# Recurrent mixer: per-head sums of squares and spreads as 64x64 products on four quarters of the matrix array

## What is computed

```python
kk = heads(k * k_k)
kk = kk / jnp.maximum(jnp.sqrt(jnp.sum(kk * kk, axis=-1, keepdims=True)), 1e-12)
...
mean = jnp.mean(y, axis=-1, keepdims=True)
var = jnp.mean(jnp.square(y - mean), axis=-1, keepdims=True)
yn = ((y - mean) * lax.rsqrt(var + RWKV_LN_EPS)).reshape(B, S, RWKV_WIDTH)
yn = yn * lnx_w.astype(f32) + lnx_b.astype(f32)
```

## Time and profile before

| what | value |
|---|---|
| time, median of 3 runs | 2650.77 us (2650.51 to 2651.02) |
| profiled execution: span from first to last instruction | 2650.5 us |
| PE / PEld / DVE / ACT busy | 2622.0 / 2259.3 / 1931.6 / 1381.8 us |
| chain that ended last, share of PE | 95% |
| mixer's core, four iterations and the end | about 291 to 449 us |

### The profile page before, as it was taken

How to read it: one execution, slowest core, us unless ns; L and a number is a source line. 1 busy time by engine, 2 the same in 40 slices (tenths; PEclk the granted TensorE clock), 3 DMA queues, 4 the chain that set the end, 5 groups by cost and what they waited for, 6 DMA issues and landing times.

```text
span 2650.5 us, 46085 instructions
## 1 busy us (share of the span) xinstructions
PE 2622.0 (99%) x16930; PEld 2259.3 (85%) x16930; DVE 1931.6 (73%) x2963; ACT 1381.8 (52%) x2153; POOL 148.1 (6%) x162
## 2 busy tenths in 40 slices
PE   9999999999999999999999999999999999999998
PEld 8888888889888888888888888888888888888886
DVE  6778676877877877878887666578877756775676
ACT  6545555676544534435554454345455535553554
POOL 5600002301000000000000000000000000000000
PEclk9999999999999999999999999999999999999999
DMA  7555103555787787878778855677665555555554
GB/s 262 174 192 175 58 4 129 181 186 215 266 300 280 285 296 278 295 281 283 278 274 304 292 177 184 203 275 281 247 206 188 194 192 189 189 194 191 188 193 151
DMA packets 159504, 578.42 MB, mean 218 GB/s; under 512 B 18224, under 2 KB 18768, under 8 KB 158288
## 3 DMA queue, kind: packets, MB, share of 16 engines
q1 hardware_dynamic: 156224, 563.59, 61.3%
q10 hardware_dynamic: 2080, 9.46, 1.0%
q0 software_dynamic: 1008, 2.71, 0.4%
HBM read 572.81 MB, written 2.11 MB: 217 GB/s over the span
## 4 chain that ended last, share of the span: by engine, by line
PE 95%; DVE 2%; issue 1%; ACT 1%; POOL 1%; DMA 0%; SPq 0%; ACTq 0%; DVEq 0%; POOLq 0%
PE ps L2742 34%; PE ps L2746 18%; PE ps L2824 12%; PE ps L2826 12%; PE ps L2825 12%; PE ps L1151 1%; PE ps L1802 1%; PE ps L1164 0%; POOL ssm L1900 0%; DMA raw<-in_stream 0%; DVE wlo L2282 0%; PE ps L1100 0%; PE ps L2808 0%; PE ps L2809 0%; PE ps L2807 0%
## 5 line engine op out<-in xcount | busy, mean ns | idle before, releaser
L2282 DVE TENSOR_TENSOR wlo<-raw,whi 128x1024 fp32r<-128x1024 f32 x872 | 1059.3, 1230 | 516.8 <-ACT whi L1933 514.1
L1933 ACT ACTIVATE whi<-raw 128x1024 fp32r<-128x1024 f32 x871 | 903.3, 1056 | 778.7 <-PE ps L2746 367.9
L2742 PE MATMUL ps<-xn,whi 128*128 128x512 f32 x3760 | 941.3, 392 | 2.7 <-DVE wi L618 1.0
L2742 PEld LDWEIGHTS ps<-xn,whi 128*128 128x128 f32 x3760 | 674.7, 188 | 123.4 <-issue 2.2
L2746 PEld LDWEIGHTS ps<-xn,wlo 128*128 128x128 f32 x3760 | 510.8, 191 | 37.4 <-DVE wlo L2282 0.4
L2746 PE MATMUL ps<-xn,wlo 128*128 128x256 f32 x3760 | 520.6, 282 | 0.0
L2824 PE MATMUL ps<-whi,act_in 128*128 128x512 f32 x1120 | 436.1, 389 | 0.0
L2826 PE MATMUL ps<-whi,act_in 128*128 128x512 f32 x1120 | 435.7, 389 | 0.0
L2825 PE MATMUL ps<-wlo,act_in 128*128 128x512 f32 x1120 | 435.7, 389 | 0.0
L2824 PEld LDWEIGHTS ps<-whi,act_in 128*128 128x128 f32 x1120 | 210.2, 188 | 44.7 <-DVE wlo L2282 1.0
L2826 PEld LDWEIGHTS ps<-whi,act_in 128*128 128x128 f32 x1120 | 210.2, 188 | 43.7
(11 more groups left out here) (344 smaller groups left out, 2233.0 us busy)
## 6 DMA issues: line engine op xcount, KB each, us to landing
raw<-in_stream SPq DMA_DIRECT2D x872, 512.0 KB, 4.2
adaw<-in_ada SPq DMA_DIRECT2D x96, 512.0 KB, 5.8
adaq<-in_ada SPq DMA_DIRECT2D x96, 512.0 KB, 5.0
h<-in_xT SPq DMA_DIRECT2D x8, 256.0 KB, 8.9
memx<-in_memT ACTq DMA_DIRECT2D x1, 2048.0 KB, 9.2
gate_row<-gates POOLq DMA_DIRECT2D x2, 1024.0 KB, 7.6
lwa<-in_lora ACTq DMA_DIRECT2D x2, 512.0 KB, 4.5
lwa<-in_lora ACTq DMA_DIRECT2D x1, 1024.0 KB, 8.6
```

The source lines that it names most:

```text
L1933: act.activation(whi[:, r, :], raw[:, r, :], ACT.Copy).then_inc(hi_done, 1)
L2282: dve.tensor_tensor(wlo[:, r, :], raw[:, r, :], whi[:, r, :].bitcast(F32), ALU.subtract)\
L2742: return pe.matmul(ps[:, lin.bank(g, t), :], whi[:, (p0 + s) % RING, c * 512 + t * P:c * 512 + (t + 1) * P], x[:, 2 * s + c, :], start=s + ...
```

## The change

Each product of 128 rows is cut into products of 64 rows by 64 columns. The array's rows used are those of head `hd` (or token half `th`), its columns those of the other one, and the eight products of a lane go round the four quarters: `quarters` lists (`b`, `hd`, `th`). Products that use different row halves write different banks, so sums and spreads now lie in two banks each instead of one. The stationary operand of the sums is 64 channels by 64 tokens with one column of ones streaming past; that of the spread is 64 tokens by 64 columns with a 64x64 identity.

Since a bank now holds part of both lanes for the key sums and for both spreads, DVE's steps and the next writer wait for both lanes. DVE reads the two banks with two instructions in place of one. The diff, cut to its core:

```diff
+    pair = lambda first, step: [first, first + step]
+    KEY_SUMS = lambda i: pair(2, 4) if i else pair(0, 2)
+    KEY_SPREAD = lambda i: pair(2, 4) if i else pair(4, 2)
+    DEV_SUMS = lambda i, g: pair(4 * g, 1 if i < 3 else 2)
+    DEV_SPREAD = lambda i: pair(3 if i < 3 else 2, 4)
+    DEV_AT = 448
...
     def norm_k_d(dve, i):
+        for z in lanes:
+            PT.wait(dve, z, i, "kn")
+            if i == 0:
+                PA.wait(dve, z, i, "gg")
         for g in lanes:
...
-            pd(dve, i, g, "km", dve.tensor_scalar(rk[2 * (i % 2) + g][:, 0:4], sums_of(i, g), 1e-24, None, ALU.max))
+            for hd in range(2):
+                ins = dve.tensor_scalar(rk[2 * (i % 2) + g][:, hd:4:2], ps[:, KEY_SUMS(i)[hd], g * P:g * P + 2], 1e-24, None, ALU.max)
+            pd(dve, i, g, "km", ins)
...
     def key_d(dve, i):
+        for z in lanes:
+            PT.wait(dve, z, i, "rb")
...
+            for t in range(2):
+                ins = dve.scalar_tensor_tensor(by_half(kk[i][g][:, :], t), by_half(tiles(n)[1], t), col("k_k", n),
+                                               spread_of(KEY_SPREAD(i)[t], g), ALU.mult, ALU.mult)
...
         def variance(i):
...
-                yd_(i, g, "ve", dve.tensor_scalar(rv[g][:, 0:4], ps[:, 4 * g, T:T + 4], 1.0 / CH, EPS_HEAD, ALU.mult, ALU.add))
+                for hd in range(2):
+                    ins = dve.tensor_scalar(rv[g][:, hd:4:2], ps[:, DEV_SUMS(i, g)[hd], DEV_AT:DEV_AT + 2],
+                                            1.0 / CH, EPS_HEAD, ALU.mult, ALU.add)
+                yd_(i, g, "ve", ins)
...
-                YT.wait(dve, g, i, "vb")
-                yd_(i, g, "yn", dve.scalar_tensor_tensor(y, y, col("lnx_w", n), spread_bank(i, g), ALU.mult, ALU.mult), True)
+                for z in lanes:
+                    YT.wait(dve, z, i, "vb")
+                for t in range(2):
+                    ins = dve.scalar_tensor_tensor(by_half(y, t), by_half(y, t), col("lnx_w", n), spread_of(DEV_SPREAD(i)[t], g),
+                                                   ALU.mult, ALU.mult)
+                yd_(i, g, "yn", ins, True)
...
+    quarters = [(b, hd, th) for b in range(2) for hd in range(2) for th in range(2)]
+
+    def head_sums(pe, banks, at_col, x):
+        for b, hd, th in quarters:
+            ins = pe.matmul(ps[rows(th), banks[hd], at_col + b:at_col + b + 1], x[rows(hd), b * P + th * CH:b * P + (th + 1) * CH],
+                            blk[rows(hd), 0, hd * CH:hd * CH + 1], start=True, stop=True)
+        return ins
...
-    def spread(pe, out, x):
-        for b in range(2):
-            for hd in range(2):
-                ins = pe.matmul(out[rows(hd), b * P:(b + 1) * P], x[:, 2 * b + hd:2 * b + hd + 1].to_broadcast([P, CH]), ident[:, :],
-                         start=True, stop=True)
+    def spread(pe, banks, g, x):
+        for b, hd, th in quarters:
+            o = g * P + b * CH
+            ins = pe.matmul(ps[rows(hd), banks[th], o:o + CH], x[rows(th), 2 * b + hd:2 * b + hd + 1].to_broadcast([CH, CH]),
+                            ident[rows(th), th * CH:(th + 1) * CH], start=True, stop=True)
         return ins
```

More of the change, by code:

```diff
@@ L340, in bank @@
         return ps[:, BANKS[i > 0][what](g), :]
[L342 to L346, removed]
+    pair = lambda first, step: [first, first + step]
[4 more added lines that the diff above has]
+    DEV_AT = 448
+    by_half = lambda x, t: x.rearrange("p (b t c) -> p t b c", b=2, t=2)[:, t, :, :]
+    spread_of = lambda bank, g: ps[:, bank, g * P:(g + 1) * P].rearrange("p (b c) -> p b c", b=2)
     def squares_k_a(act, i):
@@ L767, in norm_k_d @@
     def norm_k_d(dve, i):
+        for z in lanes:
+            PT.wait(dve, z, i, "kn")
+            if i == 0:
+                PA.wait(dve, z, i, "gg")
         for g in lanes:
-            PT.wait(dve, g, i, "kn")
-            if i == 0:
-                PA.wait(dve, g, i, "gg")
-            pd(dve, i, g, "km", dve.tensor_scalar(rk[2 * (i % 2) + g][:, 0:4], sums_of(i, g), 1e-24, None, ALU.max))
+            for hd in range(2):
+                ins = dve.tensor_scalar(rk[2 * (i % 2) + g][:, hd:4:2], ps[:, KEY_SUMS(i)[hd], g * P:g * P + 2], 1e-24, None, ALU.max)
+            pd(dve, i, g, "km", ins)
     def inverse_k_d(dve, i):
@@ L780, in key_d @@
     def key_d(dve, i):
+        for z in lanes:
+            PT.wait(dve, z, i, "rb")
         for g in lanes:
             n = 2 * i + g
-            PT.wait(dve, g, i, "rb")
-            pd(dve, i, g, "kk", dve.scalar_tensor_tensor(kk[i][g][:, :], tiles(n)[1], col("k_k", n), bank(i, g, "rb")[:, 0:T],
-                                                    ALU.mult, ALU.mult))
+            for t in range(2):
+                ins = dve.scalar_tensor_tensor(by_half(kk[i][g][:, :], t), by_half(tiles(n)[1], t), col("k_k", n),
+                                               spread_of(KEY_SPREAD(i)[t], g), ALU.mult, ALU.mult)
+            pd(dve, i, g, "kk", ins)
     def decay_sum_d(dve, i):
@@ L1029, in norm_k_t @@
             if i:
-                CA.wait(pe, g, i - 1, "zw")
-            for b in range(2):
-                ins = pe.matmul(sums_of(i, g)[:, 2 * b:2 * b + 2], kq[i][g][:, b * P:(b + 1) * P], blk[:, 0, 0:P:CH],
-                         start=True, stop=True)
-            PT.done(ins, g, "kn")
+                for z in lanes:
+                    CA.wait(pe, z, i - 1, "zw")
+            PT.done(head_sums(pe, KEY_SUMS(i), g * P, kq[i][g]), g, "kn")
     def lora_t(pe, i):
@@ L1050, in gate_t @@
             if i:
-                PD.wait(pe, g, i, "km")
+                for z in lanes:
+                    PD.wait(pe, z, i, "km")
             pe.matmul(bank(i, g, "g")[:, T:2 * T], lwa(n, 2), lora_in(1), start=True, stop=False)
             PT.done(pe.matmul(bank(i, g, "g")[:, T:2 * T], lwa(n, 3), lora_in(2), start=False, stop=True), g, "g")
-    def spread(pe, out, x):
-        for b in range(2):
-            for hd in range(2):
-                ins = pe.matmul(out[rows(hd), b * P:(b + 1) * P], x[:, 2 * b + hd:2 * b + hd + 1].to_broadcast([P, CH]), ident[:, :],
-                         start=True, stop=True)
+    def spread(pe, banks, g, x):
[3 more added lines that the diff above has]
+                            ident[rows(th), th * CH:(th + 1) * CH], start=True, stop=True)
         return ins
@@ L1065, in spread_k_t @@
             if i:
-                PA.wait(pe, g, i, "gg")
-            PT.done(spread(pe, bank(i, g, "rb")[:, 0:T], rk[2 * (i % 2) + g][:, 4:8]), g, "rb")
+                for z in lanes:
+                    PA.wait(pe, z, i, "gg")
+            PT.done(spread(pe, KEY_SPREAD(i), g, rk[2 * (i % 2) + g][:, 4:8]), g, "rb")
     def bonus_t(pe, i):
@@ L1238, in variance @@
                 YA.wait(pe, g, i, "yq")
[L1239 to L1242, removed]
+                YT.done(head_sums(pe, DEV_SUMS(i, g), DEV_AT, yq[g]), g, "va")
         def inverse(i):
@@ L1246, in inverse @@
                 YD.wait(pe, g, i, "vi")
-                YT.done(spread(pe, spread_bank(i, g), rv[g][:, 4:8]), g, "vb")
+                YT.done(spread(pe, DEV_SPREAD(i), g, rv[g][:, 4:8]), g, "vb")
         def scores(k):
```

## The result

| | before | after |
|---|---|---|
| median of 21 runs each, us | 2651.06 | 2657.90 |
| lowest and highest, us | 2649.29 to 2654.81 | 2652.87 to 2665.74 |
| ratio, 95% interval | 1 | 1.0025 [1.0019, 1.0031] |
| span of the profiled run, us | 2650.5 | 2663.9 |

The change costs 6.8 us, where 3.7 us less was forecast; the median lies 6.9 us above the top of the range. The profiled run of after is the slowest of its 21 (2665.74 us), so its trace shows more of the trouble than the median has. The runs of after spread over 13 us and go with their granted clock: 2652.9 to 2654.1 us at a mean of 0.998, 2657.9 to 2658.7 at 0.996, 2665.7 at 0.993.

What follows compares the result with a forecast made beforehand. PE was taken to bound the kernel, on the mixer's four changed steps, until DVE or ACT takes over. Terms of 0.7 + 0.75 + 1.7 + 0.2 + 0.3 = 3.65 us off 2650.77 gave 2647.1 us, range 2644.2 to 2651.0.

Steps and rivals of the forecast that it cites:

- Beside `w_in`: Tiles of `i` = 0: PE saves 0.94 us, but DVE's idle time of 0.73 caps the gain at 0.7 us.
- the first merge of iteration 0: DVE's level-2 merge in iteration 0: 0.45 us earlier from faster key sums, besides the 0.7 won earlier.
- `km`'s extra instructions: Iterations 1 and 2, chain to ACT's level-2 copy: two more instructions at `km` cost 0.14 us.
- That is the new wait of this change: Iterations 1 and 2: `lora_t` on PE waits for lane 1's `yn` from DVE, for some 0.5 us.
- The size of that wait: PE reaches `lora_t` 1.25 us earlier, DVE's `yn` only 0.25; `lora_t` starts 0.7 earlier, waiting some 0.5 us.
- Edits costed at nothing: `kk` and `yn`: DVE's `kk` and `yn` as two 128x128 steps: 0.49 us against 0.47 for one 128x256, charged nothing.
- The price of a step: Each new sum or spread on PE: 32 records at 16.6 ns, 0.53 us; 7.8 us of PE saved over four iterations.
- Slower: the thin sums let the clock fall: Rival: the clock drops after each single-column sum in three iterations, six drops at 1.6 us, 2656.7 us; chance 0.07.
- More drops: Rival: PE idles more, so the clock also falls in the tails of iterations 0 and 1, 2650.3 us; chance 0.09.
- The drop of the clock goes away: Rival: the clock drop in iteration 2's tail disappears, 1.6 us less, 2645.5 us; chance 0.22.
- All of PE's saving: Rival: waits behind DVE and ACT don't bind, so all 7.8 us arrive, 2643.0 us; chance 0.09.
- the quarters don't overlap: Rival: new records on PE follow at 33 ns, steps take 1.05 us as before, 2651.0 us; chance 0.08.

Runs made afterwards that it cites:

- fill_wait: The changed kernel plus four 128x128 products that nothing reads, ahead of the key sums in iterations 1 and 2, where PE would wait at `lora_t`: 2651.27 us.
- sums_only: The changed kernel with the old spreads and one-piece `kk` and `yn`, so only key and deviation sums are quarter products: 2649.78 us.
- sums_lora_late: sums_only with `lora_t` moved behind `doubled(i, 1)` on PE: 2649.34 us.

## Why the prediction was wrong

*What held.* The quarters overlap: from its first start to the next line's, a step of 32 records takes 0.57 to 0.76 us where PE doesn't wait behind it. By the rule of the Trainium skill that the prediction cites (page "TensorEngine Tiling (Array Packing)", section "Instruction Overhead"), as the prediction reads it, the sums would have gained nothing; this trace disagrees, 0.64 us in the chain for 1.02 at the first of them (228.60 for 228.66). Beside `w_in` 0.85 us was won (0.7 forecast); the first merge of iteration 0 is 304.56 - 303.28 = 1.28 us earlier (0.7 + 0.45 forecast); `km`'s extra instructions cost 0.35 - 0.22 = 0.13 us (0.14 forecast). The new wait was named at the right place, `lora_t` behind `yn`.

*What failed, in order of weight.*

- **"That is the new wait of this change"** was priced as lost gain only, about half a us of PE's time. Nothing was charged for the clock behind it. fill_wait shows that this one omission is the larger part of the miss, 10.8 us from the forecast to the median: filling that wait gives back 6.6 us, shorter stalls (1.9 us) included. The text had a price for a drop, 1.6 us, taken from a tail that had one, and such drops still cost 1.7. Behind `lora_t` the stretch is dense, and there one drop cost 5.1.
- **The size of that wait**: 1.04 us, 0.5 forecast. From the start of the deviation sums PE reaches `lora_t` 4.79 us later (337.01 - 332.22), 6.24 before: 1.45 us earlier, 1.25 forecast. DVE's lane-1 `yn` ends 5.69 us after that start (337.91), 5.66 before, where 0.25 earlier was forecast. So `lora_t` starts 0.41 earlier and not 0.7.
- **"Edits costed at nothing: `kk` and `yn`"**: the row taken (L810, 0.49 for two) does not read PSUM through a strided view; `yn` takes 0.60 against 0.47, two lanes 0.26 us, all that DVE was to win. `kk` grew too, 1.12 against 0.87 for both lanes, but in front of it DVE's next merge had idle time, 1.01 us now for 1.26 before.
- **Instructions were never priced.** 640 more records meant stalls of 5.3 us for 0.5. They ate the PE time that was won: without the clock's part both profiled kernels take 2646.3 to 2646.6 us, by the estimate above. The one stall of the earlier trace rows was read as an accident of that tail; it is one crossing of the same grid.
- **The price of a step**, 0.53 us, went by L1131's 16.6 ns a record. The new records follow at 14.5 to 21 ns in the mean of a step, and the steps take 0.57 to 0.76 us; by the starts a sum wins 0.2 to 0.4 us and a spread 0.3 to 0.4, some 5 us of PE in all where 7.8 were forecast.

*The rivals.* "Slower: the thin sums let the clock fall" had the sign and the clock, but the wrong cause: full clock over the thin sums in sums_only. "More drops" had the tails of iterations 0 and 1 right in this trace, at 1.7 us each, and missed the two behind `lora_t`. "The drop of the clock goes away" did happen in iteration 2's tail (no drop in after between 390 and 454), and was outweighed. "All of PE's saving" and "the quarters don't overlap" did not come true.

*What stays open.* Why one stall is followed by no drop (fill_wait, 1.21 us; after itself in iteration 2's tail, 1.04 us on issue and 1.08 on DVE), one by 3.4 us and one by 27 us at the lower level isn't settled; each kernel has one trace, so that the places of the drops in the other runs aren't known, only their sum, by the granted clock. How much of after's loss stands behind the waits of `lora_t` and how much behind the stalls varies from run to run and isn't divided. The stalls are shown to end with the loading of a block, mostly where PE used up the block ahead in 3.0 us or less, but 18 such boundaries had no stall. No version beats the kernel before beyond its interval: sums_only and sums_lora_late lie 1.5 and 2.0 us below it, with intervals that reach 1.0003 and 1.0001.

## What to carry to other kernels

When a change makes the bounding engine faster in front of a join, work out where it will wait instead, and charge for the clock behind that wait: on dense work a wait of 0.5 to 1.0 us was followed by 3.4 to 5.1 us of loss in these traces, while two of 0.3 to 0.4 us were not. A few useless products in such a wait can be the cheapest remedy; here four in each of two iterations won 6.6 us. Splitting a product into four costs four times the instructions even where its time falls, so count instructions as well as time, and read single "issue" stalls as a sign that the instruction blocks come late.

## What was not expected of the hardware

- Stalls of TensorE, 0.15 to 1.24 us, in 12 of 14 kernels, all on one grid of 256 instructions and all 1.24 to 1.57 us after an instruction packet has landed, at lines that change when 140 instructions are put in front.
- A drop to 1.2 GHz that lasts 27 us under unbroken work, behind a stall of 0.60 us, in a program whose ten other runs were 4 to 11 us shorter.
- Products of 64x64 that go round the four quarters follow one another at 14.5 to 20.5 ns in the mean of a step even with a single column, for the 33 ns of those that alternate between two.
